# Two networks of two layers on one core: paired scores and deeper lookahead in the first mixer, interleaved norm chains

## The reference

```
first network, layer l (context tokens are updated only in layer 0):
  h   = rmsnorm(x) * (1 + sc1) + sh1              # sc, sh, ga: silu(c) @ w_mod + b_mod
  p, gq, gk, gv, gg, rf, rb, aq, ak, av = split(h @ w_in)
  mix = [pool_mixer(p), gla(gq, gk, gv, rf, rb) * silu(gg), attention(aq, ak, av)] @ w_out
  x   = x + ga1 * mix
  x   = x + ga2 * relu(rmsnorm'(x) @ w_up)^2 @ w_down
then  x = rmsnorm(x, g_final)
second network, layer l:
  x   = x + gate_a * rmsnorm(mixer(rmsnorm'(x)) @ w_out)      # fox, moba and mla heads
  x   = x + gate_f * rmsnorm(swiglu(rmsnorm'(x)) @ w_down)
```

## Time and profile before

| | |
|---|---|
| median of 3 runs | 1917.11 us (1915.38 to 1918.26) |
| profiled execution | 1917.49 us, span 1915.7 us, granted clock 0.943 |
| busy, share of the span | PE 92%, PEld 73%, DVE 56%, ACT 37%, POOL 4% |
| chain that ended last | PE 78%, DVE 11%, ACT 4%, DMA 3%, issue 2%, POOL 1% |
| DMA | mean 161 GB/s; w_mod 24 loads of 2048 KB, 9.8 us to landing; w_in 12 loads, 9.0 us; w_out 8 loads, 11.0 us |
| PE waits, all | for DVE's normed rows (L1276) 31.5 + 25.8 us |

### The profile page before, as it was taken

One profiled execution on the slowest core, in us unless ns is written; L12 is line 12 of the kernel. 1 busy time (PEld: TensorE's weight loads), 2 busy tenths in 40 slices (PEclk: granted clock), 3 DMA queues, 4 the chain that ended last, 5 costly groups with the idle time before them and its releaser, 6 DMA issues.

```text
span 1915.7 us, 25661 instructions
## 1 busy us (share of the span) xinstructions
PE 1754.2 (92%) x10636; PEld 1407.9 (73%) x10636; DVE 1071.7 (56%) x1632; ACT 704.3 (37%) x878; POOL 81.5 (4%) x87
## 2 busy tenths in 40 slices
PE   4999998899999998999889996987999979779997
PEld 1786456777777777764579995675999766669996
DVE  2664456544444445654566775555666464566654
ACT  2423344321312123433544444363433243633332
POOL 0020000100000001100000001000000010010000
PEclk8999887999999999998989998988999989889999
DMA  9335870323444334358545554431554563335552
GB/s 341 113 105 198 315 260 1 108 85 137 143 151 146 132 132 145 100 182 297 207 149 202 184 181 174 174 132 58 185 176 165 192 226 115 118 110 176 177 174 90
DMA packets 172371, 309.18 MB, mean 161 GB/s; under 512 B 3264, under 2 KB 54720, under 8 KB 171616
## 3 DMA queue, kind: packets, MB, share of 16 engines
q1 hardware_dynamic: 168592, 293.98, 43.9%
q10 hardware_dynamic: 3376, 12.00, 1.7%
q0 software_dynamic: 288, 1.57, 0.2%
HBM read 305.44 MB, written 2.10 MB: 161 GB/s over the span
## 4 chain that ended last, share of the span: by engine, by line
PE 78%; DVE 11%; ACT 4%; DMA 3%; issue 2%; POOL 1%; DVEq 0%; ACTq 0%; POOLq 0%; SPq 0%
PE bank L576 60%; PE twin L576 15%; DVE ring_r L1222 3%; PE bank L585 3%; ACT arena L1950 2%; DMA ring<-in_w_mod 2%; ACT arena_r L1950 2%; DVE arena L1222 1%; DMA ring<-in_w_in 1%; POOL rs L2361 1%; DVE params L1222 1%; DVE arena L1306 1%; DVE arena_r L1222 1%; DVE X L1702 1%; DVE actT_r L1309 0%
## 5 line engine op out<-in xcount | busy, mean ns | idle before, releaser
L576 PE MATMUL bank<-arena_r 128*128 128x512 f32 (+2 forms) x2128 | 701.8, 376 | 14.3 <-DVE arena_r L1820 6.7
L1222 DVE TENSOR_TENSOR ring_r<-ring,arena_r 128x4096 fp32r<-128x4096 f32 (+4 forms) x96 | 393.9, 4103 | 218.7 <-ACT arena_r L1950 217.9
L576 PEld LDWEIGHTS bank<-arena_r 128*128 128x128 f32 x2128 | 405.1, 190 | 94.8 <-issue 8.3
L1950 ACT ACTIVATE arena_r<-ring 128x4096 fp32r<-128x4096 f32 (+4 forms) x96 | 323.5, 3370 | 377.9 <-PE bank L576 127.7
L576 PE MATMUL twin<-actT_r,arena_r 128*128 128x256 f32 x1408 | 255.6, 285 | 0.2 <-DVE actT_r L1222 0.2
L576 PE MATMUL bank<-ring_r,arena_r 128*128 128x512 f32 x624 | 245.9, 394 | 0.0
L576 PE MATMUL bank<-arena_r,actT_r 128*128 128x512 f32 (+3 forms) x624 | 217.7, 380 | 9.6 <-issue 3.3
L1950 ACT ACTIVATE arena<-bank 128x512 f32<-128x512 f32 (+6 forms) x195 | 91.9, 471 | 360.5 <-PE bank L576 276.3
L576 PEld LDWEIGHTS twin<-actT_r,arena_r 128*128 128x128 f32 x1408 | 221.2, 193 | 0.6 <-DVE actT_r L1222 0.6
L576 PE MATMUL twin<-actT_r,ring_r 128*128 128x256 f32 x704 | 200.2, 284 | 0.0
L576 PE MATMUL bank<-ring_r,actT_r 128*128 128x512 f32 (+3 forms) x496 | 182.2, 367 | 0.0
(11 more groups left out here) (191 smaller groups left out, 1681.5 us busy)
## 6 DMA issues: line engine op xcount, KB each, us to landing
ring<-in_w_mod SPq DMA_DIRECT2D x24, 2048.0 KB, 9.8
ring<-in_w_ada SPq DMA_DIRECT2D x24, 2048.0 KB, 8.6
ring<-in_w_gate_up SPq DMA_DIRECT2D x44, 1024.0 KB, 7.7
ring<-in_w_down SPq DMA_DIRECT2D x20, 2048.0 KB, 8.0
ring<-in_w_up SPq DMA_DIRECT2D x16, 2048.0 KB, 7.8
ring<-in_w_in SPq DMA_DIRECT2D x12, 2048.0 KB, 9.0
ring<-in_w_out SPq DMA_DIRECT2D x8, 2048.0 KB, 11.0
ring<-in_w_down SPq DMA_DIRECT2D x8, 1792.0 KB, 7.6
```

The costliest lines, as they stand in the source:

```text
L576: ins = nc.tensor.matmul(out_, lhsT, rhs, start=start, stop=stop)
L1222: return v.tensor_tensor(o, x, y, op)
L1950: return nc.scalar.activation(o, x, func, **kw)
```

## The change

Of the diff the parts below are left in. `scores1` now issues the scores of steps i and i + 1 together, head by head in alternation, and is called in even steps only. VectorE takes the maxima two steps ahead, reads the attended heads first in the step and one step later, and the gated stages stand at other offsets from w (`gated_scores` w + 1, `masked` w + 2, `gated_values` w + 3, `gated_turned` w + 5). The tables of steps change. `decays` works per tile, behind each product of the last w_in chunk, and its small sums go to a bank of ring s. `exponents` is cut in two parts in two steps. At the end of the first network `last_norms` does both tiles' chains in alternation, with the low part of the next weights in two halves (`split_half`) inside them; `squared` on ScalarE has the order that goes with it. `residual2` updates X per tile inside the loop and puts the low part of the next layer's w_in behind. PE's `layer2` waits for the updated X before its first fill.

```diff
+def decay_tiles(l, t):
+    return [t] if l < L - 1 else [2 * t, 2 * t + 1]
-WEIGHTED1, FILLS1 = [[1, 6, 11, 16], [1, 7]], [range(0, 14), (0, 1, 2, 3, 4, 5, 8, 9, 10, 11)]
-SUMS1, HALVES1 = [17, 6], [20, 12]
+WEIGHTED1 = [[2, 6, 10, 14], [2, 6]]
+FILLS1 = [(0, 1, 2, 3, 5, 6, 8, 9, 11, 12, 13, 15, 17, 19), (0, 1, 2, 4, 5, 6, 8, 9, 11, 13)]
+SUMS1, COLUMNS1, HALVES1 = [20, 7], [21, 13], [20, 12]
...
             def scores1(l, i):
-                heads = steps1(l)[i]
-                b, filled = take("p")
-                for n, (p, e) in enumerate(heads):
...
+                both = [(s_, take("p")) for s_ in (i, i + 1)]
+                for n in range(len(steps1(l)[i])):
+                    for s_, (b, filled) in both:
+                        heads = steps1(l)[s_]
+                        p, e = heads[n]
+                        t, hp, k0 = pairs1(l)[p]
+                        mm(b[:, 256 * n:256 * n + 512 - k0], qT[64 * e:64 * e + 64, hp, t * P:(t + 1) * P],
+                           kT[64 * e:64 * e + 64, hp // 2, k0:512], inc=filled if n == len(heads) - 1 else None)
...
                 for i in range(n + 1):
-                    if i + 2 < n:
-                        scores1(l, i + 2)
...
                     if i in FILLS1[l]:
                         fill()
+                    if i % 2 == 0 and i + 2 < n:
+                        scores1(l, i + 2)
...
-                    if j == jobs_until(l, 4):
-                        pe.wait_ge(la_ready, nth(la_ready))
-                        decays(l)
+                    if c == 4:
+                        decays(l, decay_tiles(l, t))
...
             def layer2(l):
+                pe.wait_ge(x_ready, updates("par2", l))
                 fill()
                 normed([0, 1], 2 * (L + l))
...
+            def split_half(key, part):
+                if part == 0:
+                    dve.wait_ge(whi_ready, SPLITS.index(key) + 1)
+                ks = slice(4 * part, 4 * part + 4)
+                step(tt(lower(key)[:, ks], extent(slot(key), key)[:, ks], upper(key)[:, ks].bitcast(f32), ALU.subtract),
+                     w_ready if part else v_step)
...
                 largest1(l, 0)
+                largest1(l, 1)
                 differences(l, 0)
                 for i in range(n + 1):
-                    if i + 1 < n:
-                        largest1(l, i + 1)
+                    for p in ended(l, i - 2):
+                        attended(l, p)
+                    if i + 2 < n:
+                        largest1(l, i + 2)
+                    for p in ended(l, i):
+                        inverse_sums(l, p)
                     for t in tiles:
                         w = WEIGHTED1[l][t]
+                        if i == w + 2:
+                            masked(l, t)
...
+            def last_norms(key):
+                c = slice(MODC, D)
+                for t in range(TS):
+                    b = filled()
+                    step(tt(tmpx[:, t, :], b[:, :], GA[:, t // 2, c], ALU.mult), v_emptied)
+                    step(tt(X[:, t, c], X[:, t, c], tmpx[:, t, :], ALU.add), x_ready)
+                mean_square(0)
+                split_half(key, 0)
+                mean_square(1)
+                dve.wait_ge(gf_in, 16)
+                for t in range(TS):
+                    dve.wait_ge(rstd_ready, nth(rstd_ready))
+                    step(v.scalar_tensor_tensor(out=X[:, t, :], in0=X[:, t, :], scalar=rs[:, t:t + 1], in1=gf,
+                                                op0=ALU.mult, op1=ALU.mult), x_ready)
+                mean_square(0)
+                mean_square(1)
+                for t in range(TS):
+                    dve.wait_ge(rstd_ready, nth(rstd_ready))
+                    step(v.tensor_scalar(normal(2 * L)[:, t, :], X[:, t, :], rs[:, t:t + 1], None, ALU.mult), xn_ready)
+                split_half(key, 1)
...
                         step(tt(y2[:, t, c], b[:, :], GA[:, 0, c], ALU.mult), v_emptied)
-                for t in range(TS):
-                    dve.wait_ge(rstd_ready, nth(rstd_ready))
-                    step(v.scalar_tensor_tensor(out=X[:, t, :], in0=y2[:, t, :], scalar=rs[:, t:t + 1],
-                                                in1=X[:, t, :], op0=ALU.mult, op1=ALU.add), x_ready)
+                        if half == 1:
+                            dve.wait_ge(rstd_ready, nth(rstd_ready))
+                            step(v.scalar_tensor_tensor(out=X[:, t, :], in0=y2[:, t, :], scalar=rs[:, t:t + 1],
+                                                        in1=X[:, t, :], op0=ALU.mult, op1=ALU.add), x_ready)
+                for key in late:
+                    split_half(key, 0)
                 for t in range(TS):
                     behind(t)
+                for key in late:
+                    split_half(key, 1)
```

More of the change, by code:

```diff
@@ L712, in heads, with decays @@
                     mark["qT", l, j] = k["aavv"[j]]
[L714 to L722, removed]
+            def decays(l, tiles):
+                if tiles[0] == 0:
+                    pe.wait_ge(la_ready, nth(la_ready))
+                    mark["decs", l] = take("s")
+                whole, whole_filled = mark["decs", l]
+                for t in tiles:
                     b, filled = take("a")
@@ L725, in decays @@
                     mm(b[:, 256:512], const("before16"), la[:, t, 256:512], inc=filled)
-                mark["dec", l] = k["a"] - 4
+                    mark["dec", l, t] = k["a"]
+                    for j in range(4):
+                        mm(whole[:, 4 * t + j:4 * t + j + 1], la[:, t, j * P:(j + 1) * P],
+                           const("up16")[:, P - 1:P], inc=whole_filled if t == 3 and j == 3 else None)
             def gated_heads(l):
@@ L1411, in heads, with decays @@
                 dve.wait_ge(a_emptied, mark["qT", l, 1])
-            def decays(l):
+            def decays(l, tiles):
                 ke4 = VIEWS1[l][2]
-                for t in range(4):
-                    dve.wait_ge(a_emptied, mark["dec", l] + 1 + t)
+                for t in tiles:
+                    dve.wait_ge(a_emptied, mark["dec", l, t])
                     for d in range(2):
@@ L1680, in residual2 @@
                 dve.wait_ge(ga_in, nth(ga_in, 32))
+                late = after(keys[1][-1]) if keys[1][-1][0] == "down2" else []
                 for half in range(2):
@@ L1683, in residual2 @@
                     for key in keys[half]:
-                        split(after(key))
+                        if after(key) != late:
+                            split(after(key))
                         if key == keys[half][0]:
@@ L1969, in squared @@
             def squared(tiles, n):
-                for t in tiles:
-                    for _ in range(2 if n == 2 * L else 1):
+                for _ in range(2 if n == 2 * L else 1):
+                    for t in tiles:
                         if n:
@@ L2048, in heads, with decays @@
                     step(f(qT[:, j, 0:n], b[:, 0:n], ACT.Copy), a_emptied)
-            def decays(l):
+            def decays(l, tiles):
                 ke4, dec = VIEWS1[l][2], VIEWS1[l][8]
-                b = filled()
-                step(f(dec, b[:, 0:16], ACT.Exp), a_emptied)
-                for t in range(4):
+                for t in tiles:
                     b = filled()
                     step(f(ke4[:, t, :], b[:, :], ACT.Exp), a_emptied)
+                if tiles[-1] == 3:
+                    nth(s_filled, 5)
+                    nth(s_emptied, 5)
+                    b = filled("s")
+                    step(f(dec, b[:, 0:16], ACT.Exp), s_emptied)
             def gated_heads(l):
@@ L2145, in mixer1 @@
                         w = WEIGHTED1[l][t]
-                        if i == w + 1:
+                        if i == w + 1 and t + 1 in tiles:
+                            logs(l, t + 1)
+                        if i == w + 2:
                             main_scores(l, t)
-                            if t + 1 in tiles:
-                                logs(l, t + 1)
-                        if i == w + 4:
+                        if i == w + 6:
                             gated_turned(l, t)
```

106 lines of the change are left out of this document (53 added, 53 removed).

## The result

| | before | after |
|---|---|---|
| median | 1915.1 us of 12 runs | 1925.09 us of 12 runs (1920.15 to 1929.55) |
| ratio | | 1.0044, interval 1.0029 to 1.0058 |
| profiled execution | 1917.49 us, clock 0.943 | 1920.15 us, span 1918.3 us, clock 0.945 |
| busy, share of the span | PE 92%, DVE 56%, ACT 37% | PE 90%, DVE 56%, ACT 37% |

A forecast was written before the change was run, and what follows sets the result against it. It took PE as the bound (busy 92%, chain of waits 78% PE). Mixers -24.3 and layer ends -12.3 gave -36.6 us, from 1917.49 to 1880.9 profiled, median 1880.5; own range 1873 to 1890, 8 in 10 1865 to 1904.

The forecast's parts named there:

- Lookahead: Mixers: maxima two steps ahead end ScalarE's and VectorE's waits; PE idleness falls 1.4 us in the first, 4.5 in the second.
- B: Rival: spread-out gated products hold PE at 1.2 GHz longer in the mixers; 1922 us, chance 0.07.
- Pairs: Mixers: issuing two steps' scores together saves 1.1 us per pair; 18 pairs, 19.8 us of PE work.
- rival A: PE isn't the mixers' bound; the chain sets the step and shorter products become waits; mixers -2, 1903 us, chance 0.20.
- Moved fills: Mixers: modulation products moved to later steps; -5.8 and +5.8 with 4.8 us of holes filled, and -1.9 in the second.
- Ring v: Mixers: the values product waits for VectorE's masked copy to free a buffer; 1.0 us charged for each of six tiles.
- Decays: Decays spread from one block to one tile or two per job; 0 us, bounds -0.5 and +1.5 per layer.
- C: Rival: denser work keeps PE at 2.4 GHz; another 13 us off, 1867 us, chance 0.13.
- The layer ends: Ends of both networks' layers, with norms and residuals reordered: -8.8 - 2.2 - 0 - 1.3 = -12.3 us.
- End of the first network: Both tiles' norms interleaved, so the first evacuation starts at 1170.0 instead of 1178.86; -8.8 us, bounds -5 and -10.5.
- SyncE queues the third w_in load behind it: End of first network: load issued at 1169 after the late fill lands at 1178, six us before ScalarE asks.
- rival D: End of the first network gives nothing, as the late fill or its load is asked for earlier; 1889 us, chance 0.08.

The follow-up runs named there:

- early fill: One ahead with the fill at the start of each second-network layer not waiting for X: 1879.62 us; the same on the old kernel with layer ends alone: 1907.88 us.
- one ahead: The changed kernel with VectorE's maxima taken one step ahead, as before the change, all else as changed: 1883.42 us, ratio 0.9831.
- unpaired: The one ahead kernel with each step's scores issued alone, after the fill of every step: 1898.89 us, ratio 0.9901.

## Why the prediction was wrong

**The step that failed** is *Lookahead*: "The step's maxima are taken two steps ahead ... so ScalarE's exponents no longer wait for VectorE". It counted the waits that the change takes away and not the one that it puts at the head of VectorE's queue. In an even step of the changed kernel VectorE asks for scores that PE issues in that same step, behind a fill. For PE's wait on the masked copy the prediction did name what is queued behind it, and charged 6 us (measured 4.6); it did not do so for the maxima on VectorE. There the weights, the pooled copy, the gated output and the gated norm stand behind, and PE waits for three of them by name, 34 us in all. Going back to one step is worth 2.1% (42 us), and two steps by themselves cost the old kernel 12. The prediction had looked for the next wait only in PE's queue, and its sole slower case (B) was the clock. What it said of PE's wait for the weights came true: 5.7 us of such waits in the old mixers (4.15 of them in the earlier trace rows) are gone in the changed ones.

**Once the queue is right.** The forecast for the mixers was -24.3 us; with one step ahead they are 28.6 shorter, and the kernel takes 1883.4 us, or 1879.6 with the early fill, against 1880.5 predicted. That the totals meet is in part luck. The forecast let PE's idle time fall from 19.6 to about 14 us at an unchanged clock; one ahead has 26.2 us idle, and a clock column 18.3 us lower in a fast profile makes up for it. The terms one by one:

- *Pairs:* -19.8 at most; the work fell by 17.5 to 18.7 in the changed kernel and by 14.9 from the unpaired to the paired one. In time they gave 8 us alone and 13 to 15.5 within the whole: the price of the work was right, but part of it turns into waiting, as the prediction's rival A said.
- *Moved fills:* -1.9 - 4.8, and the +5.8 and -5.8 cancel, so -6.7; measured 8.3 and 7.2 (8 and 10 by the ratios).
- *Ring v:* 6.0 charged, 4.6 measured in the changed kernel.
- *Decays:* 0 (-1.0 to +3.0); measured -3, outside the bound by its middle, not by its interval (-6.3 to -0.2).
- *Clock:* B forecast a loss, C 13 us of gain. The changed kernel is at 0.84 and 0.91 (0.83 and 0.90 before), so B did not make the loss. One ahead is at 0.92 and 0.94, and the clock column falls by 18.3 us from before, C's size. From run to run of one kernel the granted clock and the time go together, about 1 us for 0.001 of clock; one ahead runs at a mean of 0.952, the changed kernel at 0.943, so about 9 of the 42 us stand beside a higher clock. Whether the fewer gaps raise it was not tried by itself, and idle time alone does not order the clocks (unpaired: 13.5 us idle, 0.86).

**The layer ends.** -12.3 forecast, -2.9 measured as they were changed, -11.7 with the early fill. *End of the first network* is -8.8 by forecast, -9.1 by the first transposition and -8.2 by the first evacuation, which the forecast went by. *Attention ends* idle 6.55 us where it was 7.59: -1.05 each, -1.1 forecast. *Feed-forward end of the second network's first layer:* 0 by forecast; the evacuation starts 13.9 us after the last product (13.3 before), +0.6, inside the bounds. *Very end:* the span ends 7.5 us after PE's last record, 8.7 before: -1.3, as forecast; one update of X is left behind the last product, where the earlier trace rows had two in 2.60. VectorE's last row of the changed kernel:

```profile
1912.65 1.28 DVE L1748 SCALAR_TENSOR_TENSOR X<-params,rs,X 128x1024 f32<-128x1024 f32 x1
```

*What failed* is the step "SyncE queues the third w_in load behind it": the second load hangs on the fill too. In this program PE reports a matrix as read with the first product behind its last use, and behind the last w_down that product is the fill's. So SyncE issues the second load 1.1 us after the fill's start in the kernel before (1159.79) and 1.9 us after it in the changed one, 8.7 us after the last product:

```profile
1175.57 0.37 SPq L532 DMA_DIRECT2D ring<-in_w_in  x1
```

This is the load that ScalarE copies at 1183.46 in the kernel before and waits for until 1186.58 in the changed one, 11.0 us after its issue (9.0 were counted). The third load, issued at 1177.33, had its cover: the copy of it at 1195.41 doesn't wait for a transfer. Where six microseconds of cover were counted, 3.5 were lacking. That is rival D by its mechanism. A smaller loss was not listed: the transpositions now wait 0.34 and 1.11 us for VectorE, which has the second half of the low part (1.91) in front, and the first products after them have a granted clock of 0.66 (1181.6 to 1185.2), where the old kernel's had 1.00 (1182.46 to 1186.06), although its hole was longer.

**A reading of the rows.** The prediction compares the power of 10.89 us beside a subtraction with one of 7.14 us "where none did". But VectorE ran two products of 0.69 us with two inputs in SBUF beside that one as well (797.44 and 798.16 in its timeline), so the 3.75 us compare a long neighbour with two short ones. The 2.14 against 0.55 us above is the cleaner pair.

## What to carry to other kernels

Lookahead moves a wait, and the wait moves to the head of an in-order queue. Before an engine is made to ask for data earlier, look where the producer issues them, and list what stands behind the asking instruction on its own queue and who waits for that; one step of slack may be all that there is to take. Before a product is moved, ask which loads its end, and its first instruction, set going. When an edit saves busy time, add up work, clock and idle time of the stretch separately in both traces: here 17.5 of the 19.8 us of work were saved, and the loss stood in the idle column with its releasers named.

## What the runs showed of the hardware

Two steps' float32 score products of 64 rows, head by head in alternation, take 1.06 to 1.13 us for four records, against 1.12 for two (1.5 to 1.6 against 2.0 where the lower clock stretches them), and 18 such pairs lower the full-speed work of both mixers by 15 to 19 us. The granted clock of one stretch with unchanged code can differ between two executions by 0.07 (0.83 and 0.90, 9.5 us), so a few microseconds in one profile prove nothing there. A GpSimd power that took 0.55 us took 2.14 us beside a VectorE subtraction of 1.90 us with two inputs in SBUF.
